# Masking the decays and the rotary partner on VectorE, and the diagonal blocks one slot sooner

## The reference

```
# gated delta rule, one chunk of 64 tokens in the reference (the kernel uses chunks of 128)
gam = cumsum(g);  rel = gam[:, None] - gam[None, :]
decay_mat = where(incl, exp(where(incl, rel, 0)), 0)
kk    = k k^T
a_mat = where(strict, beta[:, None] * kk * decay_mat, 0)
sol   = triangular_solve(a_mat + I, [v * beta, k * beta * exp(gam)])   # unit lower triangle
qk    = (q k^T) * decay_mat
...
# rotary embedding of q and k of the differential attention, 64 channels a head
x1, x2 = x[..., :half], x[..., half:]
concatenate([x1 * cos - x2 * sin, x2 * cos + x1 * sin])     # half = 16, by row and by column
```

## Time and profile before

| | |
|---|---|
| time, 3 runs | 1965.62, 1967.37 (median), 1969.75 us |
| profiled execution | 1964.33 us, of it span 1962.5 us |
| PE busy | 1920.5 us, 98% of the span |
| DVE busy | 1393.7 us, 71% |
| ACT busy | 960.4 us, 49% |
| POOL busy | 319.7 us, 16% |
| granted TensorE clock, mean | 0.994 of full speed |

### The profile page before, as it was taken

One profiled execution on the slowest core, in us unless ns is written; L12 is line 12 of the kernel. 1 busy time (PEld: TensorE's weight loads), 2 busy tenths in 40 slices (PEclk: granted clock), 3 DMA queues, 4 the chain that ended last, 5 costly groups with the idle time before them and its releaser, 6 DMA issues.

```text
span 1962.5 us, 29026 instructions
## 1 busy us (share of the span) xinstructions
PE 1920.5 (98%) x11732; PEld 1688.5 (86%) x11732; DVE 1393.7 (71%) x1892; ACT 960.4 (49%) x1401; POOL 319.7 (16%) x499
## 2 busy tenths in 40 slices
PE   8999999999999999999999999999999999999998
PEld 8988989877888898977888888989898998998886
DVE  5686666665999989988878758665555567656665
ACT  6555656563644433444434455554434355444544
POOL 1026162533022222222221100100000000011000
PEclk9999999999999999999999999999999999999999
DMA  7455353544788888777887866755556544354563
GB/s 256 132 166 162 118 162 110 169 130 150 231 285 287 281 265 273 228 238 232 279 296 249 300 222 224 236 168 198 177 179 196 155 133 142 128 170 152 160 245 130
DMA packets 184693, 393.31 MB, mean 200 GB/s; under 512 B 12504, under 2 KB 12800, under 8 KB 183152
## 3 DMA queue, kind: packets, MB, share of 16 engines
q1 hardware_dynamic: 166672, 323.17, 50.3%
q0 software_dynamic: 17744, 68.24, 11.1%
q10 hardware_dynamic: 144, 0.07, 0.0%
HBM read 387.19 MB, written 4.23 MB: 199 GB/s over the span
## 4 chain that ended last, share of the span: by engine, by line
PE 72%; DVE 12%; POOL 5%; ACT 4%; issue 4%; DMA 2%; SPq 0%; ACTq 0%; DVEq 0%; POOLq 0%
PE GB L2084 41%; PE GB L2095 23%; DVE WL L2020 4%; DVE macc L1357 2%; POOL TB L1038 2%; POOL XB L1041 2%; DMA wm<-in_w_mod 2%; ACT WH L2015 2%; PE SB L388 1%; PE SB L1669 1%; PE SB L1770 1%; PE SB L1661 1%; PE SB L1777 1%; POOL macT L1338 1%; PE SB L751 1%
## 5 line engine op out<-in xcount | busy, mean ns | idle before, releaser
L2020 DVE TENSOR_TENSOR WL<-raw,WH 128x1024 fp32r<-128x1024 f32 x605 | 731.2, 1233 | 241.1 <-ACT WH L2015 239.4
L2015 ACT ACTIVATE WH<-raw 128x1024 fp32r<-128x1024 f32 x605 | 622.0, 1056 | 341.8 <-PE GB L2084 174.9
L2084 PE MATMUL GB<-WH,uH 128*128 128x512 f32 x896 | 282.6, 397 | 2.7 <-DVE WL L2020 2.6
L2084 PE MATMUL GB<-WH,uL 128*128 128x512 f32 x896 | 277.1, 391 | 0.0
L2084 PE MATMUL GB<-WL,uH 128*128 128x512 f32 x896 | 276.5, 390 | 0.0
L1357 DVE SCALAR_TENSOR_TENSOR macc<-wm,csil,macc 128x512 f32<-128x512 f32 x300 | 211.5, 755 | 35.4 <-DMA wm<-in_w_mod 34.1
L2095 PE MATMUL GB<-uH,WH 128*128 128x256 f32 x1280 | 214.6, 290 | 3.5 <-DVE WL L2020 2.0
L2095 PE MATMUL GB<-uH,WL 128*128 128x256 f32 x1280 | 207.1, 284 | 0.0
L2095 PE MATMUL GB<-uL,WH 128*128 128x256 f32 x1280 | 207.0, 284 | 0.0
L2084 PEld LDWEIGHTS GB<-WH,uL 128*128 128x128 f32 x896 | 168.8, 188 | 35.7
L2084 PEld LDWEIGHTS GB<-WL,uH 128*128 128x128 f32 x896 | 168.6, 188 | 35.7
(11 more groups left out here) (417 smaller groups left out, 2264.8 us busy)
## 6 DMA issues: line engine op xcount, KB each, us to landing
raw<-in_w_in SPq DMA_DIRECT2D x512, 512.0 KB, 4.5
wm<-in_w_mod POOLq DMA_DIRECT2D x96, 512.0 KB, 6.2
raw<-in_w_out SPq DMA_DIRECT2D x96, 512.0 KB, 5.6
xin<-in_x SPq DMA_DIRECT2D x4, 512.0 KB, 5.6
E<-decay_rows POOLq DMA_DIRECT2D x4, 512.0 KB, 5.6
hres<-in_x POOLq DMA_DIRECT2D x1, 2048.0 KB, 8.9
cin<-in_ctx POOLq DMA_DIRECT2D x1, 2048.0 KB, 11.8
h_spill<-hres POOLq DMA_DIRECT2D x2, 1024.0 KB, 5.1
```

What stands on the lines that cost most here:

```text
L2015: e.activation(place(s)[0][:, :, :], raw[s % NR][:, :, :], ACT.Copy).then_inc(*wh.inc("WH", s))
L2020: e.tensor_tensor(low[:, :, :], raw[s % NR][:, :, :], f32(high[:, :, :]), sub).then_inc(*wl.inc("WL", s))
L2084: m = e.matmul(banks[j][:, :], x[:, c, 128 * j:128 * j + 128], w[:, k, :], start=i == 0 and k == 0 and n == 0, stop=i == 7 and k == 1 and ...
```

## The change

1. The two mask additions on `E` move from POOL to DVE (`masked_dve`), at turn +8 for n = 0 and at turn +4 for the others.
2. The transposition to `NB` becomes a stage of its own on DVE (`blocks_dve`) at turn +11; it stood at turn +12 for n = 0, 1 and 2, and at +11 already for n = 3. ACT's copy `NTd`, for which it waits, stays where it was.
3. The plan gets half turns. Turn s + 0.5 comes behind turn s on ACT, DVE and POOL, and in the middle of the next slot's product on PE. The step of `quad` at +22 (+21 for n = 3) moves to +22.5 (+21.5). On DVE this is `X`; the generators of PE, ACT and POOL have nothing in it.
4. `perm`, its transfer and PE's matmuls with it are gone. DVE exchanges the partitions itself (`stream_shuffle` within each 32, into `att`), and all of the rotary embedding reads and writes SBUF.

```
-MASK = (4,)
+MASK, FIRST_MASK = (4,), (8,)
+BLOCKS = (11,)
-QUAD = (8, 9, 10, 12, 22, 23, 24, 25, 26, 27, 28, 29, 30, 31)
+QUAD = (8, 9, 10, 12, 22.5, 23, 24, 25, 26, 27, 28, 29, 30, 31)
...
-            e.wait_ge(*qd_act.at("nd", n))
-            if n:
-                e.wait_ge(*qd_pool.at("a30", n - 1))
-            e.transpose(NB[:, :, :].rearrange("p k r -> p r k"),
-                        NTd[:, :, :].rearrange("p m r -> p r m").unsqueeze(3).to_broadcast([128, 32, 8, 4]),
-                        ).then_inc(*qd_dve.inc("nb", n))
             yield
...
+        def blocks_dve(e, n):
+            e.wait_ge(*qd_act.at("nd", n))
+            if n:
+                e.wait_ge(*qd_pool.at("a30", n - 1))
+            e.transpose(NB[:, :, :].rearrange("p k r -> p r k"),
+                        NTd[:, :, :].rearrange("p m r -> p r m").unsqueeze(3).to_broadcast([128, 32, 8, 4]),
+                        ).then_inc(*qd_dve.inc("nb", n))
+            yield
...
-        def exponents_pool(e, n):
+        def masked_dve(e, n):
             if n == 0:
                 e.wait_ge(mask_in, 16)
             e.wait_ge(rowG_in, 16 * (n + 1))
             e.tensor_tensor(E[:, :, 256:384], E[:, :, 128:256], mask0[:, 0:128].unsqueeze(1).to_broadcast([128, 4, 128]),
-                            add).then_inc(*qe_pool.inc("ea", n))
+                            add).then_inc(*qe_dve.inc("ea", n))
...
-        def rope_pe(e, bank, k):
...
-            for b in range(2):
-                claim(e, bank, b, rp_dve.at(f"s{b}", k))
-                e.matmul(SB[b][:, :], perm[:, :], kc_part(kind, m, b), start=True, stop=True,
-                         skip_group_check=True).then_inc(*rp_pe.inc(f"p{b}", k))
+        PARTNER = [c ^ 16 for c in range(32)]
         def rope_dve(e, k):
...
-            for b in range(2):
-                e.wait_ge(*rp_pe.at(f"p{b}", k))
-                e.tensor_tensor(att[:, b, :].rearrange("p (h t) -> p h t", h=2),
-                                SB[b][:, :].rearrange("p (h t) -> p h t", h=2),
-                                sinT[:, :].unsqueeze(1).to_broadcast([128, 2, 256]), mul).then_inc(*rp_dve.inc(f"s{b}", k))
+            e.wait_ge(*kc_act.at("c", KC[kind, m]))
+            e.wait_ge(*kc_dve.at("c", KC[kind, m]))
+            turned = att[:, :, :].rearrange("p b (h t) -> p (b h) t", h=2)
+            e.stream_shuffle(turned, d, PARTNER).then_inc(*rp_dve.inc("x", k))
+            e.wait_ge(*rp_dve.at("x", k))
+            e.tensor_tensor(turned, turned, sinT[:, :].unsqueeze(1).to_broadcast([128, 4, 256]),
+                            mul).then_inc(*rp_dve.inc("s", k))
             e.tensor_tensor(d, d, cosT[:, :].unsqueeze(1).to_broadcast([128, 4, 256]), mul).then_inc(*rp_dve.inc("c", k))
...
@@ channels_pe and tokens_pe: the half turns of PE
             for k in range(2):
+                if k:
+                    take_turns(stages, s - 0.5)
...
@@ the loops over the slots of ACT, DVE and POOL
                 take_turns(stages, s)
+                take_turns(stages, s + 0.5)
```

More of the change, by code:

```diff
@@ L119, in timetable @@
 def timetable():
-    plan = {s: [] for s in range(-1, NS)}
+    plan = {s / 2: [] for s in range(-2, 2 * NS)}
     def steps(stage, first, count, rate=1.0):
@@ L135, in timetable @@
     for n in range(4):
-        at(("mask", n), end("qkv", 3 * n + 2), MASK)
+        at(("mask", n), end("qkv", 3 * n + 2), MASK if n else FIRST_MASK)
         at(("exp", n), end("qkv", 3 * n + 2), EXP)
         at(("quad", n), end("qkv", 3 * n + 2), QUAD if n < 3 else QUAD3)
+        at(("blocks", n), end("qkv", 3 * n + 2), BLOCKS)
     for k in range(12):
@@ L206, in hybrid_program @@
         Y5 = sb("Y5", [128, 8, 32])
-        perm = sb("perm", [128, 128])
         cosT = sb("cosT", [128, 256])
@@ L350, in hybrid_program @@
         fold_in = sem("fold_in")
-        mask_in, unit_in, perm_in, cos_in, sin_in, nmask_in, lam_in = (
-            sem(n + "_in") for n in ("mask", "unit", "perm", "cos", "sin", "nmask", "lam"))
+        mask_in, unit_in, cos_in, sin_in, nmask_in, lam_in = (
+            sem(n + "_in") for n in ("mask", "unit", "cos", "sin", "nmask", "lam"))
         raw_in = [sem(f"raw_in{b}") for b in range(NR)]
@@ L672, in hybrid_program @@
         qd_pe = steps("qd_pe", "tv0", "tv1", "k0", "k1", "k2", "k3", "y5", "z5", "y6", "z6", "w", "r", "u", "o0", "o1")
-        qe_pool, qe_act = steps("qe_pool", "ea", "eb"), steps("qe_act", "E")
+        qe_dve, qe_act = steps("qe_dve", "ea", "eb"), steps("qe_act", "E")
         qd_act = steps("qd_act", "vt0", "vt1", "nd", "y5", "z5", "y6", "z6", "W", "q", "ln", "rs")
@@ L2087, in tokens_pe, with channels_pe @@
             return m
-        def channels_pe(e, unit, s, banks):
+        def channels_pe(e, unit, s, banks, stages):
             i, (wh_, wl_) = SLOTS[s][1], place(s)
             for k in range(2):
+                if k:
+                    take_turns(stages, s - 0.5)
                 H, L, c = moving(unit, 2 * i + k)
@@ L2230, in _ @@
             stages.update({("cv", r): conv_dve(e, r) for r in range(12)})
+            stages.update({("mask", n): masked_dve(e, n) for n in range(4)})
             stages.update({("quad", n): quad_dve(e, n) for n in range(4)})
+            stages.update({("blocks", n): blocks_dve(e, n) for n in range(4)})
             stages.update({("ml", hf): mlstm_dve(e, hf) for hf in range(2)})
@@ L2254, in _ @@
             for dst, name, done in ((mask0[:, :], "c_mask0", mask_in), (unit_cols[:, :, :], "c_unit", unit_in),
-                                    (perm[:, :], "c_perm", perm_in), (fold[:, :], "c_fold", fold_in), (cosT[:, :], "c_cos", cos_in),
+                                    (fold[:, :], "c_fold", fold_in), (cosT[:, :], "c_cos", cos_in),
                                     (sinT[:, :], "c_sin", sin_in), (nmask[:, :], "c_nmask", nmask_in),
@@ L2264, in _ @@
             stages.update({("quad", n): quad_pool(e, n) for n in range(4)})
-            stages.update({("mask", n): exponents_pool(e, n) for n in range(4)})
             take_turns(stages, -1)
@@ L2289, in _ @@
             stages.update({("ml", hf): ml_pe(e, bank, hf) for hf in range(2)})
-            stages.update({("rope", k): rope_pe(e, bank, k) for k in range(4)})
             take_turns(stages, -1)
             for s in range(NS):
-                product_pe(e, s)
+                product_pe(e, s, stages)
                 take_turns(stages, s)
+            take_turns(stages, NS - 0.5)
 def _constants(np):
@@ L2305, in _constants @@
     c = np.arange(128)
-    perm = np.zeros((128, 128), f)
-    perm[c ^ 16, c] = 1.0
     fold = (c[:, None] % 32 == c[None, :] % 32).astype(f)
@@ L2318, in _constants @@
     nmask = np.where((k >= c0) & (k < c0 + 16), f(0), f(NEG)).astype(f)
-    return dict(c_ident=ident, c_mask0=mask0, c_unit=unit, c_perm=perm, c_fold=fold, c_cos=cosT, c_sin=sinT, c_nmask=nmask)
+    return dict(c_ident=ident, c_mask0=mask0, c_unit=unit, c_fold=fold, c_cos=cosT, c_sin=sinT, c_nmask=nmask)
 def kernel(**inputs):
```

29 lines of the change are left out of this document (11 added, 18 removed).

## The result

The changed kernel takes 1958.73 us (median of 7 runs, 1956.92 to 1962.6) beside 1968.38 us for the kernel before on the same chip (median of 7): a ratio of 0.995, 95% interval 0.9941 to 0.9959, or 9.65 us less. The forecast was 1955, the range 1946 to 1962.

The account below looks back on a forecast made before the run. PE, busy 1920.5 of 1962.5 us, was taken to set the time. Gains of 1.6 (vv) + 2.6 (waits) + 3.2 (clock) + 5.2 (rotary) = 12.6 us gave 1951.7 profiled, 1955 as median; range 1946 to 1962.

Parts of the forecast that it names:

- The collision and the moved waits: Rounds 0 to 2: POOL's multiplication delays DVE's qk, PE's waits move from z5 to y5; net gain 2.6 us.
- rival (a): No collision: DVE's qk gets its turn before POOL's, y5 waits 0.4 us each; median 1947 us; chance 22%.
- The wait for vv: Round n = 0: with the mask off POOL, PE's wait for the convolution vv goes; gain 1.6 us.
- The clock: Slow matmuls at half clock behind the z5 waits cost 4.8 us; two thirds counted as gained, 3.2 us.
- rival (b): Waits at y5 and z5 only move, as long as before, and the clock falls behind each; 1961 us; chance 14%.
- Round 3 "doesn't change": Round n = 3 keeps its 2.98 us wait at y5, with full clock behind it, since neither NB nor X moves there.
- The rotary embedding: PE loses two matmuls, 1.72 us, at four places; three gain, the fourth gains 0: 5.2 us in all.
- The wait at the first scores: At the fourth rotary embedding PE comes 1.7 us sooner but waits until the same moment, about 2 us; gain 0.
- The mask's cost: DVE's two mask additions per round take 1.9 us, covered by 3.7 us of slack before PE takes R; cost 0.
- rival (c): Mask additions on DVE cost 4.2 us and more, so R reaches PE late in three rounds; 1972 us; chance 6%.

Follow-up runs that it names:

- e4_turn: Changed kernel, with POOL's multiplication of qk by the norms also waiting until VectorE has written that round's other qk: 1945.99 us, ratio 0.9894 to the kernel before.
- e1_rope: Kernel before with the rotary part of the change alone (VectorE's shuffle, no matmul with perm): 1963.88 us, ratio 0.9982.
- e2_mask: Kernel before with the mask additions alone moved to VectorE: 1963.52 us, ratio 0.9981.
- e3_rounds: Kernel before with only NB at +11 and X at +22.5 (+21.5 for n = 3), mask still on POOL: 1966.64 us, ratio 1.0004.
- e7_again: The changed kernel once more, unaltered, for a second profile: 1956.36 us, ratio 0.9954 to the kernel before.
- e9_nb_late: Changed kernel with NB back at +12 for rounds 0 to 2: 1951.22 us, ratio 0.9929 to the kernel before.
- e5_last: e4_turn with round n = 3's steps from y5 on one slot later on all engines, X and XT unmoved: 1945.74 us, ratio 0.9898 to the kernel before.
- e6_scores: e4_turn with the attention's first two steps at turns 3 and 5 instead of 2 and 4: 1942.95 us, ratio 0.9882 to the kernel before.
- e12_before: The kernel before once more, unaltered, for a second profile: 1967.82 us for this one execution.
- e10_both: e6_scores with round n = 3's X at +22.5, XT at +23 and all later steps one slot later: 1941.23 us, ratio 0.9873 to the kernel before.

## Why the prediction was right, and where it was not

**The collision and the moved waits (2.6 us): right.** POOL's multiplication was put 0.16 us behind the start of the split of round 0 (175.4 against 175.24); it came 0.20 behind (172.32 against 172.12). Only who goes first was the other way: not the split and then POOL, but POOL and then the split. So `qk` took 1.21 us directly behind the split, which the prediction had named as the sign of rival (a), and the 3.7 us are the split's; the collision is there all the same. The sum of the three operations is the same (5.7 us from the start of the split to `y5`), and so are the waits at `y5`: forecast 2.7, 2.0, 2.7, measured 2.68, 1.91, 2.66. Net of the old waits that is 2.7 us. `NB` started 2.57 us sooner against its split, as forecast (142.37 - 138.67 before, 136.66 - 135.53 now). e4_turn shows that the turn is the cause. Rival (a), no collision, is what e4_turn then made: waits of 0.19 us where it said 0.4, and 1945.99 us where it said 1947.

**The wait for vv (1.6): right in place.** It is gone in every kernel with the mask on VectorE. The part alone measured 3.7 us (2.0 to 5.3), of which 2.1 go with a higher clock. One place for that is the old wait itself, behind which e1_rope's profile has a fall; how often that happens, no run here shows.

**The clock (3.2 us): the term that was mis-sized; over the whole execution it measured 0.0.** The reason given was that a wait at `y5` had left the clock alone in n = 3 while all three at `z5` had not. This was one execution read as a rule. The mean granted clock is on record for every execution, not for the profiled ones alone. In the kernel before, a thousandth of it goes with some 2 us: the 15 executions at 0.993 took 1969.0 us on average, the 16 at 0.995 took 1965.3. With this price, an estimate, the clock and what the traces show of waits and of PE's matmuls can be added up for each kernel (us against the kernel before, in brackets the number of executions):

| kernel | mean granted clock | clock | waits and matmuls | together | measured |
|---|---|---|---|---|---|
| before | 0.9940 (55) | | | | |
| e1_rope | 0.9938 (11) | +0.4 | -5.1 | -4.7 | -3.5 |
| e2_mask | 0.9951 (11) | -2.1 | -1.6 | -3.7 | -3.7 |
| e3_rounds | 0.9934 (12) | +1.2 | -1.7 | -0.5 | +0.8 |
| changed, e7_again | 0.9940 (12) | 0.0 | -9.4 | -9.4 | -9.65, -9.0 |
| e9_nb_late | 0.9960 (6) | -3.9 | -11.6 | -15.5 | -14.0 |
| e4_turn | 0.9968 (5) | -5.5 | -16.1 | -21.6 | -20.9 |

From the scatter of the executions, the clock of the changed kernel is level with the old one to 1.2 us either way, so a gain of 3.2 is ruled out. This half of rival (b), that the clock falls as before, came true; the other half, waits as long as before, did not. e4_turn gained more than the 6.7 us of its waits because the clock does come back there: 5.5 us by its five executions, which alone are few (4 us either way), and 5.7 (1.7 either way) by the 13 of e4_turn, e5_last and e6_scores, which have the same waits of 0.19 us in rounds 0 to 2.

Where the clock falls, only the profiles tell, each for one execution. The time from `y5` to `y6`, with all waits in it taken off (the differences of PE's starts, as for e7_again above), is:

| kernel | n = 0 | n = 1 | n = 2 | n = 3 |
|---|---|---|---|---|
| before | 8.90 | 8.94 | 9.54 | 7.14 |
| e12_before | 8.95 | 8.94 | 9.60 | 9.77 |
| e1_rope (old order) | 8.93 | 7.44 | 8.82 | 8.71 |
| e2_mask (old order) | 9.53 | 7.44 | 8.77 | 8.75 |
| e3_rounds (new order) | 8.87 | 7.45 | 8.76 | 7.14 |
| after | 7.38 | 8.86 | 10.03 | 9.83 |
| e7_again | 8.88 | 7.40 | 7.14 | 8.71 |
| e4_turn (waits of 0.19) | 7.43 | 7.43 | 7.33 | 9.75 |
| e6_scores (waits of 0.19) | 7.43 | 7.43 | 7.32 | 8.75 |

A stretch at full clock takes 7.1 to 7.5 us, one with a fall 1.4 to 2.9 more. Rounds 0 to 2 together average 26.5 us in the four executions of the old order (25.2 to 27.5) and 24.9 in the three of the new (23.4 to 26.3). These seven are too few: the two groups overlap, and the difference of 1.5 us is not shown. There are falls in 10 of 12 stretches of the old order and in 5 of 9 of the new, so the rounds may well get something back that is lost at other places, such as the scores (below); that stays open. Where the waits are 0.19 us, the clock did not fall in any of the six stretches here, nor in the six of e5_last and e10_both.

**Round 3 "doesn't change": right for the wait, not for the clock.** The wait varies between 2.88 and 3.32 us in kernels old and new. The first profile of before happened to have no fall there, and that of the changed kernel had one of 2.7 us.

**The rotary embedding (5.2 us): right.** 5.14 us in the pair of profiles and 5.16 in e1_rope's; 1.8 to 5.1 by the runs of the part alone, so the forecast lies at the edge there. The wait at the first scores was forecast at about 2 us and is 2.04; in two of seven executions with it, e4_turn and e7_again, the next step on PE then came 1.5 us later (8.4 us behind the scores instead of 6.9), which the sum did not have. The shuffle took 1.32 us where 1.2 was taken. The prediction's estimate of 1.2 us, half of what the Trainium skill ("VectorE: DVE Perf Modes", The perf-mode tier table) gives for 2048 elements, is thus 10% low. Halving is what made it low at least in part: on DVE here half the columns cost more than half the time (0.68 us for the mask addition of 512 columns, 1.23 for that of 1024).

**The mask's cost (0): right.** The additions take 1.9 us, and `R` had no new wait in any round; rival (c) is out.

**The sum.** Without the clock's 3.2 the forecast of 12.6 us is 9.4: 1.6 + 2.7 + 5.1, against 9.65 and 9.0 (0.9954 of 1966.75) measured. The forecast of 1955 missed 1958.73 by 3.7 us, 3.0 of them in this sum and 1.0 because the kernel before took 1968.38 in the comparison and not 1967.37. The profiled pair showed only 5.9, since the profile of before was a favourable execution: beside e12_before it had 2.6 us less in round 3 and 2.6 less between 850 and 1100 us, and only 1.7 more at a fall of the clock near its start. Beside e12_before (1967.82) the changed kernel's profile is 9.4 shorter. The loss between 850 and 1100 us comes from VectorE, which waits there for the transfer `wm`, as shown here for one place. In the first profile of before, in e12_before and in the changed kernel (DVE, start, us, idle before):

```profile
1090.77 1.54 DVE L1357 SCALAR_TENSOR_TENSOR macc<-wm,csil,macc 128x512 f32<-128x512 f32 x2 [3.72 <-DMA wm<-in_w_mod]
```

```profile
1094.21 1.54 DVE L1357 SCALAR_TENSOR_TENSOR macc<-wm,csil,macc 128x512 f32<-128x512 f32 x2 [5.69 <-DMA wm<-in_w_mod]
```

```profile
1090.00 1.54 DVE L1363 SCALAR_TENSOR_TENSOR macc<-wm,csil,macc 128x512 f32<-128x512 f32 x2 [6.42 <-DMA wm<-in_w_mod]
```

The splits behind it are late, and PE's waits for `WL` in its products with 512 columns sum to 2.6, 4.8 and 5.1 us. e7_again, the same kernel as the last, has 3.4, and e1_rope 6.1. So kernels old and new have this loss in sizes that overlap, and nothing shows it as a price of the change. What decides the length of that transfer wasn't tried.

## What to carry to other kernels

When VectorE and GpSimd share turns, ask for each GpSimd operation of 2 us not how long it takes but which VectorE operation it will stand in front of; making its input ready sooner can make the kernel slower. One wait between them, for which GpSimd sat idle 2.3 us, gave more (11 to 12 us) than the whole change (9.65). And one profile tells the length and place of most waits to 0.1 us, but not whether the clock falls behind them in the next execution. For that, compare the mean granted clock over many executions of both kernels before a term of the sum rests on it.

## What the runs showed of the hardware

- A VectorE split recorded as begun at 172.12 lost its turn to a GpSimd multiplication recorded at 172.32 and took 3.71 us; at 359.11 and 359.30 it was the same (3.69 us). With GpSimd's operation recorded 0.94 us behind the start of the split (264.22 and 265.16, e9_nb_late), the split kept its 1.23 us, and the next VectorE operation was held (3.41 us). But the recorded starts alone do not tell who gets the turn: in the kernel before, with GpSimd's operation recorded 0.08 and 0.09 us behind the split (175.24 and 175.32; 119.39 and 119.48), the split kept its turn and GpSimd was the one held. What decides it, no run here shows. The split of the second pair:

```profile
119.39 1.23 DVE L2020 TENSOR_TENSOR WL<-raw,WH 128x1024 fp32r<-128x1024 f32 x1 [2.09 <-ACT WH L2015]
```

- A 32x32 transposition on VectorE kept its 1.80 us beside GpSimd's multiplication (177.46 and 177.69, e4_turn).
- In the rows of the table of `y5` to `y6`, the granted clock fell to 1.2 GHz behind each of eight waits of PE of 3.8 to 3.95 us and of five of 3.32 us; behind waits of 1.9 to 3.0 us it fell in some executions and not in others, of the same kernel too; behind waits of 0.19 us it fell in none of 12 stretches (six of them in e5_last and e10_both). A thousandth of the mean granted clock went with some 2 us of 1967.
- The exchange of partitions within each 32 took 1.32 us for 1024 float32 columns, 0.1 more than a multiplication of the same size.
